# Layer 1's gate projection on Trainium2: fifteen units as seven half-size products, with weight sums built by accumulating transfers

## What is computed

```python
def merge_branches(branches, gate_logits, w_branch, w_out):
    gates = jax.nn.sigmoid(gate_logits)
    merged = gates[..., :D_MODEL] * (branches[0] @ w_branch[0])
    for i in range(1, N_BRANCH):
        merged = merged + gates[..., i * D_MODEL:(i + 1) * D_MODEL] * (branches[i] @ w_branch[i])
    return merged @ w_out
```

## Time and profile before

| | before |
|---|---|
| median of 3 runs | 2863.29 us (2861.12 to 2864.88) |
| profiled execution | 2864.46 us |
| its span | 2862.6 us |
| TensorE busy | 2722.6 us, 95% of the span |
| VectorE, ScalarE, GpSimd busy | 1350.7, 436.0, 75.4 us |
| moved by the DMA engines | 685.48 MB, mean 239 GB/s |

### The profile page before, as it was taken

The page is one execution under the profiler, slowest core; times in us unless marked ns, Lnnn a source line. Parts: engine busy times, 40 slices in busy tenths (PEclk is TensorE's granted clock), DMA queues, the critical chain, the costliest instruction groups (busy, mean ns, idle before and its releaser), DMA issues.

```text
span 2862.6 us, 42389 instructions
## 1 busy us (share of the span) xinstructions
PE 2722.6 (95%) x17586; PEld 1977.2 (69%) x17586; DVE 1350.7 (47%) x2753; ACT 436.0 (15%) x873; POOL 75.4 (3%) x137
## 2 busy tenths in 40 slices
PE   7999999998899899999988998899999999999998
PEld 3544444576666567788644444488788998988997
DVE  3856656442222233785411111179734764843763
ACT  0222220210000012231100000011422211122110
POOL 0100002000000000000100000000000000000000
PEclk9999999999999999999999999999999999999999
DMA  9623339379999985233899999954232444333441
GB/s 377 202 103 122 122 128 356 121 317 421 420 407 421 421 348 165 100 115 148 331 421 421 420 384 421 421 203 160 100 134 104 175 163 147 135 140 116 162 162 45
DMA packets 114765, 685.48 MB, mean 239 GB/s; under 512 B 20752, under 2 KB 22032, under 8 KB 39712
## 3 DMA queue, kind: packets, MB, share of 16 engines
q1 hardware_dynamic: 84144, 600.79, 53.1%
q0 software_dynamic: 16992, 69.54, 6.7%
q10 hardware_dynamic: 13456, 12.59, 1.7%
HBM read 679.46 MB, written 3.41 MB: 239 GB/s over the span
## 4 chain that ended last, share of the span: by engine, by line
PE 37%; DMA 14%; DVE 1%; issue 0%; ACT 0%; SPq 0%; DVEq 0%; ACTq 0%
PE ps L780 14%; DMA ring<-units 14%; PE ps L752 11%; PE ps L1527 2%; PE ps L1346 2%; PE ps L1222 2%; PE ps L1488 1%; DMA early_values<-arena 1%; PE ps L1358 0%; PE ps L1378 0%; PE ps L1088 0%; PE ps L815 0%; PE ps L789 0%; PE ps L798 0%; PE ps L1276 0%
## 5 line engine op out<-in xcount | busy, mean ns | idle before, releaser
L1222 PE MATMUL ps<-ring,arena 128*32 128x256 f32 x2928 | 359.8, 382 | 45.9 <-DMA ring<-units 44.4
L1207 PE MATMUL ps<-ring,arena 128*64 128x256 f32 x2960 | 339.3, 381 | 45.3 <-DMA ring<-units 45.1
L1207 PEld LDWEIGHTS ps<-ring,arena 128*64 128x64 f32 x2960 | 227.0, 137 | 148.7 <-issue 65.5
L1222 PEld LDWEIGHTS ps<-ring,arena 128*32 128x32 f32 x2928 | 175.2, 109 | 222.5 <-DMA ring<-units 90.9
L752 PE MATMUL ps<-h,ring 128*128 128x256 f32 (+1 forms) x992 | 246.0, 408 | 3.2 <-ACT h L1706 2.1
L1047 PE MATMUL ps<-u,ring 128*128 128x512 f32 (+1 forms) x544 | 235.1, 586 | 0.5 <-DVE arena L2345 0.5
L752 PEld LDWEIGHTS ps<-h,ring 128*128 128x128 f32 x992 | 186.7, 190 | 61.3 <-issue 34.7
L1047 PEld LDWEIGHTS ps<-u,ring 128*128 128x128 f32 x544 | 102.6, 191 | 126.7 <-issue 125.1
L2681 DVE COPY u<-ps 32x512 f32<-32x512 f32 (+1 forms) x128 | 70.9, 554 | 209.9 <-PE ps L1222 116.9
L752 PE MATMUL ps<-arena,ring 128*128 128x256 f32 x640 | 139.5, 379 | 1.3 <-DVE arena L3115 1.3
L752 PEld LDWEIGHTS ps<-arena,ring 128*128 128x128 f32 x640 | 121.4, 190 | 18.1 <-DVE arena L3008 1.7
(11 more groups left out here) (501 smaller groups left out, 3958.3 us busy)
## 6 DMA issues: line engine op xcount, KB each, us to landing
ring<-units SPq DMA_DIRECT2D x568, 1024.0 KB, 13.4
slots<-turned_mod POOLq DMA_DIRECT2D x62, 512.0 KB, 5.2
arena<-turned_mod POOLq DMA_DIRECT2D x18, 512.0 KB, 11.2
arena<-quarters ACTq DMA_DIRECT2D x32, 256.0 KB, 2.9
arena<-units POOLq DMA_DIRECT2D x7, 1024.0 KB, 7.2
h<-tokens SPq DMA_DIRECT2D x4, 512.0 KB, 12.2
arena<-neighbours ACTq DMA_DIRECT2D x32, 64.0 KB, 8.8
arena<-tokens ACTq DMA_DIRECT2D x1, 2048.0 KB, 14.2
```

Of the source, the lines that this page charges most:

```text
L1207: last = nc.tensor.matmul(ps[j * slots:(j + 1) * slots, bank, lo:lo + UC], lhsT[:, kt, 0:slots], row_of(w[j], kt), start=(kt == 0), stop=( ...
L1222: last = nc.tensor.matmul(ps[j % 4 * slots:(j % 4 + 1) * slots, banks[j // 4], 0:UC], lhsT[:, kt, 0:slots], row_of(w[j], kt), start=(kt == ...
```

## The change

In layer 1, chunks 1 to 15 compute their gate unit as seven products of half size in each dimension (`gate_products`): outputs, inputs and tokens are each cut into two halves, and four matmuls of 128x128 weights by 256 columns make a product. Two products use plain blocks, the others sums of blocks. The sums over tokens are made once, by VectorE in chunk 0, into ring slots 4 and 5. The sums over weights are made by GpSimd's transfers from a second copy of the gate units in DRAM (`gate_blocks`): block A is copied four times side by side (1,024 KB), block B is added to the first three places (768 KB), block C to the last three (768 KB), and block D to the third (256 KB). Each transfer waits for the one before. Two sets, in ring slots 6 and 7, serve odd and even chunks; a set is free when TensorE is done with the unit two before. So the ring has four slots for units 16 to 34, and eight again from unit 35 on, behind the last merge.

VectorE puts the quarters of the gate together (`early_blocks`, `add_fifth`, `late_blocks`), ScalarE keeps the first product (`first_product_kept`) and applies the hyperbolic tangent in place when all are added. `MOD_MIX` is new: 2 and 3 tiles in turn, then 2, 3, 6, 6, 5, and 15 behind the last merge. GpSimd issues the tiles between the chains of transfers.

```diff
-MOD_MIX = (1,) + 10 * (3,) + (3, 10, 10, 9, 0)
+MOD_MIX = (1,) + 5 * (2, 3) + (2, 3, 6, 6, 5)
+GATES, NARROW = 15, 35
+def slot_of(n):
+    return n % (RING // 2) if GATES < n < NARROW else n % RING
...
+def blocks_of_gates(units):
+    w = units[GATES + 1:GATES + 16].reshape(15, P, 2, 4, 2, P)
+    return np.stack([w[:, :, 0, :, 1], w[:, :, 1, :, 1], w[:, :, 0, :, 0], w[:, :, 1, :, 0]], 1).reshape(60, P, 4 * P)
...
+            for n in range(2 * RING, NARROW + 5):
+                if n < 2 * RING + RING // 2:
+                    sp.wait_ge(units_used, n - RING + 1)
+                elif n <= NARROW:
+                    sp.wait_ge(units_used, n - RING // 2 + 1)
+                else:
+                    sp.wait_ge(merged_step, 16)
+                sp.dma_start(ring[:, slot_of(n), :], units[n]).then_inc(loaded[n % RING], 16)
...
-            modulation_tiles(0, MOD_LATE + MOD_SLOTS)
-            pool.wait_ge(mixed, 24)
-            modulation_tiles(MOD_LATE + MOD_SLOTS, MOD_TILES)
+            used = sum(MOD_PREPARE)
+            issued = used + MOD_SLOTS
+            modulation_tiles(0, issued)
+            for chunk in range(15):
+                c = chunk + 1
+                to = wide_weight_sets[c % 2]
...
+                pool.wait_ge(units_used, max(GATES + c - 1, GATES))
+                pool.dma_start(to[:, 0:4, :], blocks(0, 4)).then_inc(wide_weights_copied, 16)
+                pool.wait_ge(wide_weights_copied, 16 * c)
+                pool.dma_start(to[:, 0:3, :], blocks(1, 3), accum_op=ALU.add).then_inc(wide_fourth_added, 16)
+                pool.wait_ge(wide_fourth_added, 16 * c)
+                pool.dma_start(to[:, 1:4, :], blocks(2, 3), accum_op=ALU.add).then_inc(wide_first_added, 16)
+                pool.wait_ge(wide_first_added, 16 * c)
+                pool.dma_start(to[:, 2, :], ap["gate_blocks"][chunk * 4 + 3], accum_op=ALU.add).then_inc(wide_weights_summed, 16)
+                used += MOD_MIX[chunk]
+                upto = min(used + (MOD_SLOTS if used < MOD_LATE else len(tile_slots)), MOD_TILES)
+                if issued <= MOD_LATE + MOD_SLOTS < upto:
+                    pool.wait_ge(mixed, 24)
+                modulation_tiles(issued, upto)
+                issued = upto
+            modulation_tiles(issued, MOD_TILES)
...
+                def gate_products(c):
+                    w = unit()
+                    s, t = wide_weight_sums[c % 2], wide_token_sums
...
+                    pe.wait_ge(gate_kept, 2 * c)
+                    product(gb + 1, 0, w[:, 0:4, 0:P], u[:, 0:4, 0:S]).then_inc(wide_first_ready, 1)
+                    product(gb, 0, w[:, 4:8, 0:P], u[:, 4:8, 0:S])
+                    pe.wait_ge(wide_tokens_summed, 1)
+                    pe.wait_ge(wide_first_added, 16 * c)
+                    product(gb, 1, s[1], t[1]).then_inc(wide_early_ready, 1)
+                    attend(2 * c)
+                    pe.wait_ge(merged_step, c)
+                    product(wb + 1, 1, s[0], t[0]).then_inc(wide_fifth_ready, 1)
+                    product(wb, 1, s[3], t[2])
+                    pe.wait_ge(wide_weights_summed, 16 * c)
+                    product(wb, 0, s[2], u[:, 4:8, S:]).then_inc(wide_late_ready, 1)
+                    pe.wait_ge(wide_fifth_added, c)
+                    product(wb + 1, 0, w[:, 4:8, P:UC], t[3]).then_inc(units_used, 1)
...
+                    elif l == 0:
+                        pe.wait_ge(gates_added, chunk)
...
+                        exps(2 * chunk)
+                        act.wait_ge(wide_first_ready, chunk)
+                        A(first_product_kept, ps[:, gb + 1, 0:S], ACT.Copy).then_inc(wide_first_kept, 1)
+                        next_quarter(chunk)
+                        copies(2 * chunk)
+                        exps(2 * chunk + 1)
+                        copies(2 * chunk + 1)
+                        count.skip(units_used, 1)
+                        act.wait_ge(gates_added, chunk)
+                        A(gate[:, :, 0:T], gate[:, :, 0:T], ACT.Tanh, scale=0.5).then_inc(gate_kept, 2)
...
+                def early_blocks(chunk):
+                    dve.wait_ge(merged_step, chunk)
+                    dve.wait_ge(wide_first_kept, at(wide_first_kept))
+                    dve.wait_ge(wide_early_ready, at(wide_early_ready))
+                    link(v.tensor_tensor(gate[:, :, 0:S], ps[:, gb, :].rearrange("p (a n) -> p a n", n=S),
+                                         wide(first_product_kept, [P, 2, S]), ALU.add))
...
+                def late_blocks():
+                    dve.wait_ge(wide_fifth_added, at(wide_fifth_added))
+                    dve.wait_ge(wide_late_ready, at(wide_late_ready))
+                    link(v.tensor_tensor(gate_blocks[:, S:3 * S], gate_blocks[:, S:3 * S], ps[:, wb, :], ALU.add))
+                    dve.wait_ge(units_used, at(units_used))
+                    count.skip(units_used, -1)
+                    link(v.scalar_tensor_tensor(fourth, third, -1.0, ps[:, wb + 1, S:], ALU.mult, ALU.subtract))
+                    v.scalar_tensor_tensor(third, third, -1.0, ps[:, wb + 1, 0:S], ALU.mult, ALU.subtract).then_inc(gates_added, 1)
...
-                        softmax(2 * chunk + 1)
+                        if chunk:
+                            early_blocks(chunk)
+                            softmax(2 * chunk + 1, add_fifth)
+                            late_blocks()
+                        else:
+                            softmax(2 * chunk + 1)
...
                 merge(15)
+                if l == 0:
+                    modulation_tiles(MOD_TILES - sum(MOD_PREPARE) - sum(MOD_MIX), 16)
```

More of the change, by code:

```diff
@@ L363, in build @@
         rtmp = part(10752, 4, S)
+        wide_token_sums = [part(1024 * (i % 2), 4, S, of=ring[:, 4 + i // 2, :]) for i in range(4)]
+        wide_weight_sets = [part(0, 4, 4 * P, of=ring[:, 7 - q, :]) for q in range(2)]
+        wide_weight_sums = [[part(4 * P * i, 4, P, of=ring[:, 7 - q, :]) for i in range(4)] for q in range(2)]
+        gate_blocks = gate.rearrange("p j n -> p (j n)")
+        first_product_kept = small[:, 512:512 + S]
         merged = [h, h[:, :, S:]]
@@ L704, in unit_at @@
                 pe_wait_unit(n)
-                return ring[:, n % RING, :].rearrange("p (k c) -> p k c", c=UC)
+                return ring[:, slot_of(n), :].rearrange("p (k c) -> p k c", c=UC)
             def pe_wait_unit(n):
@@ L1017, in attend, with product @@
                         scores(i + 1)
+                def gate_products(c):
+                    w = unit()
+                    s, t = wide_weight_sums[c % 2], wide_token_sums
+                    def product(bank, half, lhsT, rhs):
+                        for k in range(4):
+                            last = nc.tensor.matmul(ps[:, bank, half * S:(half + 1) * S], lhsT[:, k, :], rhs[:, k, :],
+                                                    start=(k == 0), stop=(k == 3))
+                        return last
+                    pe.wait_ge(gate_kept, 2 * c)
[12 more added lines that the diff above has]
+                    product(wb + 1, 0, w[:, 4:8, P:UC], t[3]).then_inc(units_used, 1)
                 steps = 2 if l == 0 else 1
@@ L1026, in mix_branches @@
                     done = 16 * l + chunk
-                    sevens = l == 1 and chunk > 0
-                    if sevens:
+                    if l and chunk:
                         if chunk == 1:
@@ L2488, in merge, with add_fifth @@
                         v.tensor_tensor(m, m, t, ALU.add).then_inc(merged_step, 1)
+                first, second, third, fourth = [gate_blocks[:, n * S:(n + 1) * S] for n in range(4)]
+                def early_blocks(chunk):
[4 more added lines that the diff above has]
+                                         wide(first_product_kept, [P, 2, S]), ALU.add))
+                def add_fifth():
+                    dve.wait_ge(wide_fifth_ready, at(wide_fifth_ready))
+                    v.tensor_tensor(second, third, ps[:, wb + 1, S:], ALU.add).then_inc(wide_fifth_added, 1)
+                def late_blocks():
[6 more added lines that the diff above has]
+                    v.scalar_tensor_tensor(third, third, -1.0, ps[:, wb + 1, 0:S], ALU.mult, ALU.subtract).then_inc(gates_added, 1)
                 for chunk in range(16):
@@ L3143 @@
     }
+    arrays["gate_blocks"] = blocks_of_gates(arrays["units"])
     arrays = {k: np.ascontiguousarray(v) for k, v in arrays.items()}
```

45 lines of the change are left out of this document (32 added, 13 removed).

## The result

| | before | changed kernel |
|---|---|---|
| median of the runs | 2863.2 us | 2972.9 us (2970.5 to 2984.7, 4 runs) |
| ratio to before | | 1.0392, 95% interval 1.0364 to 1.042 |
| profiled execution, its span | 2864.46, 2862.6 us | 2972.48, 2970.7 us |
| stage, to the start of the output projection | 487.96 us | 595.53 us |
| TensorE busy in the stage, mean granted clock | 340.4 us, 1.00 | 349.4 us, 0.88 |

The kernel became 109.7 us slower, 3.9%; 2873.1 was forecast, with 2910 as the upper end. The span grew by 108.1 us and the stage by 107.6, so the whole loss lies in the gate stage.

The account below looks back on a forecast made before the run. TensorE was taken to bound the gate stage. Without the chain, -24.0 + 5.6 + 2.5 + 8.0 = -7.9 us; chain-bound at P = 20.4, +9.8 us instead, giving 2873.1 us; range 2849 to 2910.

Parts of the forecast that it names:

- P: Gate stage: time for a chain's three awaited transfers to land, put between 16.8 and 21.9 us, taken as 20.4.
- part 4: Gate stage: the serial chain of weight-sum transfers sets the pace beyond P of about 19.2 us; +9.8 us at 20.4.
- W: Gate stage: the chain's own wait for tiles to be taken, about 4 us at chain 3 and 4 at tiles 51 to 53.
- the doubled price: Transfer chain: an accumulating transfer needs its data time twice, 2.55 us more for 768 KB, making P 21.9 us.
- the plain bound: Transfer chain: accumulating transfers cost no more than plain ones, 4.25 us for 768 KB standing alone, making P 16.8 us.
- Hand-overs: Transfer chain: passing from one awaited transfer to the next, 0.3 us within P.
- Rival (d): Transfer chain: an accumulating transfer costs three times the data time or more, P = 27.0, about 2965 us; chance 0.08.
- Rival (a): Transfer chain: accumulates go at nearly the plain rate and the chain stays out of the way, -7.9 us, 2855.4; chance 0.30.
- Part 1: TensorE's gate products: 12.2 us a unit instead of 13.84, 1.6 us saved in each of 15 units, -24.0 us.
- Part 2: VectorE's assembly of the gate: 1.4 us exposed in each of chunks 12 to 15, +5.6, and 2.5 for long chunks.
- Part 3: Late modulation tile 51 at chunk 13: TensorE waits for the merge, 8.0 us for P = 16.8.
- The tail: Behind the gate stage: 15 tiles on VectorE after the last merge, 18 us, hide with 7 us to spare.

Follow-up runs that it names:

- e3: Changed kernel with the three accumulating transfers left out, only the copy kept (weight sums missing from the output): 2843.7 us.
- e6: Changed kernel with the modulation tiles issued in thirds between the chain's transfers instead of all behind the fourth: 2932.9 us.
- e2: Changed kernel with the first transfer of each chain, the copy, issued by SyncE instead of GpSimd: 2921.6 us.
- e10: Changed kernel with 3 modulation tiles each in chunks 13 to 15 instead of 6, 6 and 5, and 23 behind the last merge: 2989.6 us.
- e9: Kernel of e8 with 3 modulation tiles in each of the last three chunks instead of 6, 6 and 5, and 23 behind the last merge: 2894.6 us.
- e1: Changed kernel with the three accumulating transfers made plain ones of the same sizes (weight sums missing from the output): 2885.6 us, one run.
- e8: Changed kernel with the accumulates made plain and the modulation tiles issued between the transfers (weight sums missing): 2882.6 us.
- e7: Kernel of e4 with GpSimd's additions moved behind the second softmax, and tiles freed in a chunk's first half issued ahead of them: 2852.1 us.
- e4: Changed kernel with the weight sums made by four GpSimd additions from the unit in the ring instead of the transfers: 2864.5 us.
- e5: Kernel of e4 with VectorE's scaling of the row maxima written as a two-operand scalar_tensor_tensor: 2864.5 us.

## Why the prediction was wrong, step by step

**What failed: P.** The formula of part 4 held. With the measured P it gives 190.8 + 14 x 27.15 + 8 = 578.9 us for the third transfer of chain 15, and GpSimd's timeline has it at 579.62. (W was put at 8, half of it at chain 3; there it is nothing, and it is 8.4 at tiles 51 to 53.) The projection follows 15.9 us later, 13.4 in the working: behind the last wait 24 records take 8.0 us, where e3 has 5.2. But P was put at 20.4 and between 16.8 and 21.9, and it is 27.15. Term by term against the doubled price:

- The copy: 5.3 and 0.9 for other traffic were taken, 10.0 measured, **+3.8**. This is the mis-sized term. It was costed from a copy that stands alone in its queue, and the 0.9 from tiles that mostly did too. In the new order the copy stands behind the fourth accumulate and two or three tiles of its own queue. The working counted the time to issue these, 1.3 us, but not their bytes ahead of the copy. e6 and e2 show it: moved from behind them it lands in 8.2 and 6.3 us (6.2 had been taken), and behind nine tiles in 17 (e10) and 22 (e9).
- The accumulates: 7.7 each at the doubled price, measured 8.0 and 7.5. The forecast took 0.7 of the step from plain to doubled, 6.9 each: **+1.6** over the two. e1 shows that the plain bound was right for plain transfers, 4.8 and 5.1 against 5.15.
- Hand-overs: P less the three median landings is 27.15 - 25.5 = 1.65, taken 0.3, **+1.35**. It is a remainder, and no run takes it apart.

Together they are the 6.75 us missing; fourteen chains make 94.5 of the 98 us between the forecast start of the projection and the measured one.

The Trainium skill's rule ("Collectives: The Full Stack", section "The bandwidth ceiling: the fold count and why AG ≠ RS ≠ AR"), half the copy rate for a transfer that reduces, agrees with the row: 2.4 to 3.2 us more on 768 KB against 2.55 estimated. It priced the addition rightly. The result lies some 78 us above what the rule gave here: P is 5.25 us above the 21.9, of which 3.8 are the copy's place in its queue and 1.35 the hand-overs, and of these the rule says nothing.

**Rival (d)** gave nearly the right time, P = 27.0 and 2965, by the wrong mechanism, which is luck: no accumulate cost three times its data. **Rival (a)** was wrong in its own condition. At the plain price, in e1, P is 20.5, above the 19.2 that the working itself gave as the point from which the chain decides.

**Part 1, fewer columns: right.** Where nothing is awaited the products of a unit follow at

```profile
188.51 3.62 PE L1087 MATMUL ps<-u,ring 128*128 128x256 f32 x16
191.97 1.89 PE L1087 MATMUL ps<-ring 128*128 128x256 f32 x8
...
196.03 3.72 PE L1087 MATMUL ps<-ring 128*128 128x256 f32 x16
199.59 1.89 PE L1087 MATMUL ps<-u,ring 128*128 128x256 f32 x8
201.31 1.89 PE L1087 MATMUL ps<-ring 128*128 128x256 f32 x8
```

or 3.46 + 1.73 + 3.56 + 1.72 + 1.73 = 12.2 us a unit.

**Part 2: right, a little high.** The wait before the branch products in the last chunks is 1.1 us, 1.4 forecast. In e3 parts 1 and 2 together give -21.8 us in the stage against -15.9; part of that is that the 2.5 us charged for the long chunks do not show.

**Part 3: right mechanism, wrong size.** VectorE waited 21.7 us for tile 51, and TensorE 15.5 us behind it in chunk 14, forecast 8.0. (VectorE also waited 18.0 us for tiles one chunk before, which no step had; TensorE stood 3.3 us behind that.) The 8.0 was for P = 16.8; by its own formula P = 25.8 in that chain gives 17. Taking it away doesn't shorten the stage by as much, as e10 shows: 2.3 us.

**The tail: right.** The first wait behind the projection stands 34.3 us after its start as before, with 15 tiles hidden. e10 shows that the cover ends soon behind them.

**What no step had:** TensorE's records are slower behind most of its waits. At 328.55, behind 9.43 us of idle time, eight records take 3.75 us where 1.89 is usual; behind 2.58 us at 271.74 they take 1.97. That the chain would make TensorE idle was said; that idling would also cost 34 us of busy time was not. Since the chain sets the end, most of it must be hidden in the same waits: the formula without it came out right but for the last 2.8 us.

## What to carry to other kernels

Cost a transfer in a serial chain by all that its queue holds at its issue: the bytes of what was issued just before it, not only the time to issue them. A chain of dependent transfers with an awaited landing in each link wants nothing else in its queue but what fits between the links; in e8 even one tile there made a link longer, 6.7 us instead of 5.1. Before using a transfer to add, look for an engine that can add from where the operands lie already: four additions of 1.27 us replaced 27 us of chain, and then the place of the additions against VectorE's stream decided between no gain (2864.5) and 0.4% (2852.1).

## What the runs showed of the hardware

- **An accumulating transfer** of 768 KB lands in 7.5 to 8.0 us and a plain one in 4.8 to 5.1, in the same place and with the same shapes; its issue takes 1.28 against 0.76 us. With the copies in another queue (e2) it lands in 11.8.
- **A transfer lands later behind others of its queue.** The 1,024 KB copy landed in 5.6 us in the first chain, with nothing issued in its queue for 6 us, in 10.0 behind an accumulate and two or three tiles, in 6.3 from another queue (e2), and in up to 22 behind nine tiles.
- **VectorE and GpSimd exclude each other by operand.** VectorE operations with two SBUF operands, and the scaling by a constant, were held while GpSimd added from SBUF (0.17 to 3.96 us), those with a PSUM operand were not (0.69 and 0.42 us beside the additions of e7). The Trainium skill says so ("SBUF — State Buffer", section "Who interferes with whom"): a VectorE instruction with two SBUF inputs, or in a two-port mode, contends with a GpSimd instruction that reads SBUF, one with at most one SBUF input outside these modes does not. The rows of e4, e5 and e7 agree. Of the two-port modes it says too that whoever issues first has the ports for the whole instruction and the other is blocked. In e4 the hold spans three additions in a row, and in e7 tile and addition are both stretched, to 2.28 and 2.25 us.
- **The clock behind waits.** With 103.5 us of idle time in the stage TensorE's granted clock was 0.88 over it, with 8.4 (e3) it was 1.00. The stretch behind the wait of 9.43 us has a clock of 0.50, the lower level of 1.2 GHz, and its records took twice their usual time:

```profile
328.55:332.10 3.55, 3.55 (x9) 2.73 (x9) 0.00 (x0) 0.00 (x0) 3.27 (x5) 0.50 0.49 88
```
